# Attention's values in two products a head instead of three, with the dilated half's division on ScalarE

## The chip, the cores and the metric

The kernel runs on one core of a Trainium2 chip. The metric is the device time of one execution in microseconds. The engines are TensorE (PE in the profile, its weight loads PEld), VectorE (DVE), ScalarE (ACT), GpSimd (POOL) and SyncE (SP), which starts DMAs. Each engine takes its own instructions strictly in the order of its list; semaphores tie the lists together.

## The reference

The program is two network blocks, one behind the other, on 512 tokens of width 1024. The change touches the attention of the first block alone: 8 heads of causal attention with a forget gate ("fox") and 8 heads of dilated attention, 64 values wide each. Cut to that part:

```python
proj = rms_norm(h, norm1_g) @ w_in                 # q, k, v of both kinds of heads
# fox, per head: causal softmax over all keys before
s = q @ k.T / 8 + c_q - c_k ; p = softmax(mask(s)) ; fox_out = p @ v
# dilated, per head: three windows (128 by 1, 512 by 4, 2048 by 16), each a softmax
# with an ALiBi bias, mixed by their denominators
o = sum_i softmax_i(lse)[i] * (softmax(s_i) @ v)
h = h + concat(fox_out, dil_out) @ w_out
```

The rest (a layer of 16384 small experts, then retention, convolution and a gated layer) runs behind it and isn't changed.

## The kernel before

**Numbers in two parts.** Products are made in fp32r. So that little is lost, an operand is split in a high part (ScalarE's copy into fp32r) and a low part (the original less the high part, by VectorE or, for some weights, GpSimd), and a product A B is three matmuls: high high, high low, low high. Lines 1351 to 1353 are the three of a projection's weight tile: `wh`, `wl` are a weight's parts (ScalarE makes `wh` from the loaded `raw`, line 2539; `wl` is line 1826 on VectorE or 2941 on GpSimd), `XH` and `XL` those of the normed input.

**Units and groups.** Weights come in units of 128 output features by 1024, 8 tiles of three matmuls each. Units 1 to 24 make q, k, v for eight groups of two heads (groups 0 to 3 are dilated, 4 to 7 fox); units 25 to 32 are the output projection `w_out`, which reads the heads' results from `MH` and `ML` (high and low part, one slot of 512 columns for a group, `place(g)`, 64 partitions for each head).

**Attention beside it.** One generator, `timeline()`, yields the pieces of work; each engine runs through it and issues its share, so the order of every list is fixed when the program is built. Attention is side work: after each tile of the projection a tick lets `attend()` go on by its credit (its yields of 1.4 and 1.35 for the first 34 of its iterations, 1.05 after), that is 2.75 tiles an iteration and later 2.1. It has 64 steps n: group, head, block qb of 128 queries, with 128 (qb + 1) keys. Iteration n issues, in this order:
- `turn_low` of step n-4: VectorE takes the low part of the transposed probabilities into `PTL`, from PSUM, and frees that bank (P4 or P5);
- `scores` n: TensorE, three matmuls into one of three banks;
- `soft` n-1: VectorE adds the mask in place and takes the row minimum (line 1969), ScalarE the exponential into one of five tiles T (line 2668; 2670 for fox heads, which also sums);
- `normal` n-2: VectorE multiplies by the counts of windows that see a key (`CNT`) and sums (line 1979, dilated heads only), takes the reciprocal (line 1983) and multiplies by it (line 1985);
- a tile or two of the projection;
- where step n-5 was the fourth of its head, `values` of that head (lines 1618 to 1632): 12 matmuls into P6, then ScalarE copies 64 rows to `MH` and VectorE takes `ML`;
- `turn` n-3: TensorE transposes the probabilities (line 1358) and ScalarE copies them to `PTH`, the high part;
- a tile or two.

`VV` holds the values of a group's two heads, 4 key blocks of 128 columns (64 for each head), the high part in one tensor, the low part in another; so a product for one head also computes the other head's 64 rows, which nobody reads. The V of a group is copied out of its bank (`v_copy`), transposed (`v_turn`) and split; Q and K are split from their banks (`qk_split`). These pieces stand at the end of units, ahead of or behind `attend()`'s pieces as the ticks fall. `high` and `low` are the weight pieces of units to come, up to four ahead. The waits in the lists: VectorE's low part waits for ScalarE's `PTH` copy (`s_pth`), ScalarE's exponential for VectorE's minimum (`s_min`), the count product for the exponential (`s_exp`), the transposes for the division (`s_soft`), output tiles for `ML` (`s_ml`).

## Time and profile before

| | |
|---|---|
| runs | 2445.4, 2454.4, 2445.06 us; median 2445.4 |
| the profiled execution | 2445.81 us, span 2443.6 us |
| TensorE's granted clock, mean | 0.997 of full speed |
| busy share of the span | TensorE 99%, VectorE 73%, ScalarE 48%, GpSimd 23% |

In the page's 40 slices of 61 us attention lies in the first to the fifth. The granted clock is 90% or more of full speed in each slice. Busy shares are averages over stages with different limits; a wait belongs to the engine named first, and the engine behind the arrow ended it. A matmul's recorded end is modelled and overlaps the next one's start, so distances between starts say more of TensorE than durations.

### The profile page before, as it was taken

How to read it: one execution, taken by the hardware profiler on the slowest of the kernel's cores; microseconds unless marked ns; L12 is line 12 of the kernel's file. 1: busy time of each engine (PE TensorE's matmuls, PEld its weight loads, DVE VectorE, ACT ScalarE, POOL GpSimd, SP SyncE). 2: the span in 40 equal slices, each digit the busy share in tenths (PEclk: the TensorE clock that was granted, in tenths of full speed). 3: DMA queues.
4: the chain of work that ended last, by engine and by line, in shares of the span. 5: the costliest groups of instructions: out<-in, count | busy, mean ns of one | idle time of the engine just before them, and what ended most of it. 6: DMA issues, size and time to landing. Idle time of an engine off the chain costs nothing.

```text
span 2443.6 us, 35669 instructions
## 1 busy us (share of the span) xinstructions
PE 2408.1 (99%) x13533; PEld 2189.5 (90%) x13533; DVE 1781.7 (73%) x3391; ACT 1185.1 (48%) x2193; POOL 564.7 (23%) x372
## 2 busy tenths in 40 slices
PE   8999999999999999999999999999999999999998
PEld 7788888999999999999999998887888888888887
DVE  7876667998998886899999988777785336433323
ACT  6555466478778885333333345445322223332222
POOL 3222065133333541455555510000000000000000
PEclk9999999999999999999999999999999999999999
DMA  4111345699999999999999972222574322222331
GB/s 173 67 57 53 122 147 177 218 325 342 344 336 341 389 405 363 411 412 412 411 407 409 410 286 83 81 87 93 183 250 134 104 87 95 95 98 93 106 101 35
DMA packets 193114, 533.89 MB, mean 218 GB/s; under 512 B 16712, under 2 KB 65896, under 8 KB 190768
## 3 DMA queue, kind: packets, MB, share of 16 engines
q1 hardware_dynamic: 151472, 380.60, 43.3%
q0 software_dynamic: 41472, 151.01, 16.2%
q8 instruction: 108, 1.77, 0.3%
q14 instruction: 62, 0.51, 0.1%
HBM read 480.09 MB, written 51.46 MB: 218 GB/s over the span
## 4 chain that ended last, share of the span: by engine, by line
PE 91%; DVE 4%; ACT 2%; DMA 1%; issue 1%; DVEq 0%; SPq 0%; ACTq 0%
PE P L1351 28%; PE P L1353 28%; PE P L1352 28%; PE P L1716 2%; DMA hdram<-HID 1%; PE P L1358 1%; ACT wh L2539 1%; DVE wl L1826 1%; DVE T L1829 0%; PE P L1631 0%; PE P L1630 0%; PE P L1629 0%; PE P L1608 0%; PE P L1609 0%; PE P L1607 0%
## 5 line engine op out<-in xcount | busy, mean ns | idle before, releaser
L1351 PE MATMUL P<-XH,wh 128*128 128x512 f32 (+2 forms) x2272 | 833.9, 367 | 3.7 <-DVE wl L1826 3.7
L1353 PE MATMUL P<-XH,wl 128*128 128x512 f32 (+2 forms) x2272 | 817.6, 360 | 0.0
L1352 PE MATMUL P<-XL,wh 128*128 128x512 f32 (+2 forms) x2272 | 817.3, 360 | 0.0
L2539 ACT ACTIVATE wh<-raw 128x1024 fp32r<-128x1024 f32 x458 | 482.5, 1056 | 398.4 <-PE P L1353 398.4
L1826 DVE TENSOR_TENSOR wl<-raw,wh 128x1024 fp32r<-128x1024 f32 x422 | 512.6, 1223 | 84.5 <-ACT wh L2539 81.5
L1351 PEld LDWEIGHTS P<-XH,wh 128*128 128x128 f32 x2272 | 428.0, 188 | 48.2 <-DVE wl L1826 4.7
L1353 PEld LDWEIGHTS P<-XH,wl 128*128 128x128 f32 x2272 | 427.4, 188 | 47.6
L1352 PEld LDWEIGHTS P<-XL,wh 128*128 128x128 f32 x2272 | 428.2, 188 | 42.7 <-issue 1.9
L1351 PE MATMUL P<-AH,wh 128*128 128x368 f32 (+1 forms) x1024 | 337.4, 330 | 1.1 <-DVE AL L1826 1.1
L1352 PE MATMUL P<-AL,wh 128*128 128x368 f32 (+1 forms) x1024 | 336.7, 329 | 0.0
L1353 PE MATMUL P<-AH,wl 128*128 128x368 f32 (+1 forms) x1024 | 336.7, 329 | 0.0
L2990 POOL DMA_INDIRECT GV<-vt,SI x128 | 201.3, 1573 | 172.5 <-DVE SUM L1829 152.3
L2981 POOL DMA_INDIRECT GB<-un,SI x116 | 159.3, 1374 | 285.1 <-DVE HS L2172 231.8
L1351 PEld LDWEIGHTS P<-AH,wh 128*128 128x128 f32 x1024 | 192.4, 188 | 1.6 <-issue 1.4
L1352 PEld LDWEIGHTS P<-AL,wh 128*128 128x128 f32 x1024 | 192.4, 188 | 0.0
L1353 PEld LDWEIGHTS P<-AH,wl 128*128 128x128 f32 x1024 | 192.4, 188 | 0.0
L1826 DVE TENSOR_TENSOR T<-P,T 128x512 f32<-128x512 f32 x47 | 32.5, 691 | 197.0 <-PE P L1353 191.8
L1829 DVE SCALAR_TENSOR_TENSOR SUM<-GV,HS,SUM 128x1024 f32<-128x1024 f32 x127 | 162.6, 1281 | 4.0 <-DVE SUM L1829 0.5
L2172 DVE CUSTOM_DVE_ANT_0 GB<-GB,XT 128x1024 f32<-128x1024 f32 x116 | 140.6, 1223 | 14.0 <-DMA GB<-un,SI 13.9
L2752 ACT ACTIVATE OM<-OE,GTL 128x128 f16<-128x128 f16 x368 | 146.2, 436 | 0.0
L2941 POOL TENSOR_TENSOR wl<-raw,wh 128x1024 fp32r<-128x1024 f32 x36 | 86.4, 2399 | 249.5 <-ACT wh L2539 248.0
L2776 ACT ACTIVATE HID<-P 128x368 f32<-128x368 f32 x128 | 60.8, 475 | 95.7 <-PE P L1353 82.7
(345 smaller groups left out, 3393.9 us busy)
## 6 DMA issues: line engine op xcount, KB each, us to landing
raw<-wts SPq DMA_DIRECT2D x211, 512.0 KB
raw<-ut SPq DMA_DIRECT2D x128, 512.0 KB
raw<-vt SPq DMA_DIRECT2D x128, 512.0 KB
hdram<-HID SPq DMA_DIRECT2D x64, 384.0 KB
HI<-hdram SPq DMA_DIRECT2D x32, 768.0 KB
gdram<-GS SPq DMA_DIRECT2D x23, 1024.0 KB
GI<-gdram SPq DMA_DIRECT2D x16, 1472.0 KB
AWC<-adat SPq DMA_DIRECT2D x64, 256.0 KB, 5.4
```

The costliest lines, as they stand in the source:

```text
L1351: e.matmul(bank, wh[:, w], H, start=start, stop=False)
L1352: e.matmul(bank, wh[:, w], L, start=False, stop=False)
L1353: return e.matmul(bank, wl[:, w], H, start=False, stop=stop)
L1826: return e.tensor_tensor(dst, a, b, op)
L1829: return e.scalar_tensor_tensor(out=dst, in0=a, scalar=scalar, in1=b, op0=op0, op1=op1)
L2172: e.tensor_tensor_reduce(out=b[:, :], in0=b[:, :], in1=rows_[:, :], scale=1.0, scalar=0.0, op0=ALU.mult, op1=ALU.add, accum_out=sums[:, k: ...
L2539: return e.activation(dst, src, ACT.Copy)
L2752: t = e.activation(OM[n % 2][:, 1, r, :, o], OE[n % 3][:, 0, r, :, o], ACT.Copy, scale=GTL[n // 32 % 2][:, at_:at_ + 1])
L2776: e.activation(HID[n % 2][:, i % 2, NX:ND], P[i % 4][:, NX:ND], ACT.Gelu).then_inc(s_gelu, 1)
L2941: e.tensor_tensor(WL[i % NW][:, :], RAW[i % NRAW][:, :], WH[i % NW][:, :].bitcast(F32), ALU.subtract).then_inc(s_low_p, 1)
L2981: e.indirect_dma_start(GB[n % 4][:, :], None, un, bass.IndirectOffsetOnAxis(ap=(SIX if extra else SI)[:, k:k + 1], axis=0)).then_inc(d_row ...
L2990: e.indirect_dma_start(GV[n % 6][:, :], None, table, bass.IndirectOffsetOnAxis(ap=(SIX if extra else SI)[:, k:k + 1], axis=0)).then_inc(d_ ...
```

## The change

It has four parts.

1. `VV` becomes `VX`: for each key block and head 64 columns of the high part and, right beside them, 64 of the low part. One wide matmul with both as weights and `PTH` moving gives high high in rows 0 to 63 of P6 and low high in rows 64 to 127; a narrow one with 64 columns of weights and `PTL` moving adds the third product to rows 0 to 63. So 8 matmuls a head. The last head (v = 15) keeps three products, all with 64 columns.
2. The two halves of P6 are added: ScalarE copies rows 0 to 63 to `MS` (tile T5), VectorE adds rows 64 to 127 to it. An iteration later (`values_high`) ScalarE copies `MS` to `MH` and GpSimd subtracts for `ML`. The last head goes the old way.
3. `T5` is now `MS`, so V waits for its transposes in one tile (`T6`) instead of two.
4. For steps of the dilated heads the multiplication by the reciprocal goes from VectorE to ScalarE (`normal` in ScalarE's part, line 2709 in the changed program).

```diff
@@ -361,11 +361,13 @@
                 yield ("soft", n - 1, *steps[n - 1])
             if 0 <= n - 2 < ns:
                 yield ("normal", n - 2, *steps[n - 2])
+            if 0 <= n - 6 < ns and steps[n - 6][2] == 3:
+                yield ("values_high", *steps[n - 6][:2])
+                state["values"] += 1
             yield 1.4 if n < 34 else 1.05
             if 0 <= n - 5 < ns and steps[n - 5][2] == 3:
                 g, h, _ = steps[n - 5]
                 yield ("values", g, h, at[n - 5], v_at[g])
-                state["values"] += 1
             if 0 <= n - 3 < ns:
                 at[n - 3] = tr()
                 yield ("turn", n - 3, *steps[n - 3], at[n - 3])
...
@@ -881,7 +883,7 @@
         MH = at("MH", F + 16, [128, 8, T], F32R)
         ML = at("ML", F + 32, [128, 8, T], F32R)
         QK = [[at(f"QK{g}{i}", F + 48 + 16 * g + 4 * i, [128, 2, T], F32R) for i in range(4)] for g in range(2)]
-        VV = [[at(f"VV{g}{i}", F + 80 + 4 * g + 2 * i, [128, 4, 128], F32R) for i in range(2)] for g in range(2)]
+        VX = [at(f"VX{g}", F + 80 + 4 * g, [128, 4, 2, 2, 64], F32R) for g in range(2)]
         hT = at("hT", F, [128, 8, T], F32)
         adr = nc.dram_tensor("adram", [2, 8, T], F32, kind="Internal").ap()
         cd = nc.dram_tensor("cdram", [2, 8, T], F32, kind="Internal").ap()
...
@@ -956,6 +958,7 @@
         DM = [at(f"DM{i}", F + 94 + 2 * i, [128, T], F32) for i in range(2)]
         RSQ = at("RSQ", F + 98, [128, T], F32)
         R1 = TB[4]
+        MS = TB[5]
 
 
         AWC = [at(f"AWC{i}", F + (16, 18, 20, 22, 28, 30)[i], [128, T], F32) for i in range(6)]
...
@@ -1591,7 +1596,7 @@
                     p.wait_ge(s_tr[t % 2], t // 2)
                 elif t == 0:
                     p.wait_ge(s_fox_v, 1)
-                transposes(P[4 + t % 2], TB[6 - g % 2], 4).then_inc(s_vt, 1)
+                transposes(P[4 + t % 2], TB[6], 4).then_inc(s_vt, 1)
 
             def scores(n, g, h, qb):
                 q = QK[g % 2]
...
@@ -1618,17 +1623,34 @@
             def values(g, h, t, tv):
                 v = 2 * g + h
                 if v:
-                    p.wait_ge(s_ml, v)
+                    p.wait_ge(s_mix, 3 * v - 1)
                 else:
                     p.wait_ge(s_vcopy, 2)
                 p.wait_ge(s_tr[t % 2], t // 2 + 1)
                 p.wait_ge(s_tr[tv % 2], tv // 2 + 1)
-                vh, vl = VV[g % 2]
+                both = VX[g % 2]
                 for kb in range(4):
-                    d = P[6][:, kb * 128:T]
-                    e.matmul(d, vh[:, kb, :], key_row(PTH, v, kb), start=kb == 0, stop=False)
-                    e.matmul(d, vh[:, kb, :], key_row(PTL, v, kb), start=False, stop=False)
-                    m = e.matmul(d, vl[:, kb, :], key_row(PTH, v, kb), start=False, stop=kb == 3)
+                    d = slice(kb * 128, T)
+                    if v < 15:
+                        def wide():
+                            return e.matmul(P[6][:, d], both[:, kb, h, :, :].rearrange("p a b -> p (a b)"),
+                                            key_row(PTH, v, kb), start=kb == 0, stop=kb == 3)
+
+                        def narrow():
+                            return e.matmul(P[6][0:64, d], both[:, kb, h, 0, :], key_row(PTL, v, kb), start=False,
+                                            stop=False)
+
+                        if kb < 3:
+                            wide()
+                            narrow()
+                        else:
+                            narrow()
+                            m = wide()
+                    else:
+                        e.matmul(P[6][0:64, d], both[:, kb, h, 0, :], key_row(PTH, v, kb), start=kb == 0, stop=False)
+                        e.matmul(P[6][0:64, d], both[:, kb, h, 1, :], key_row(PTH, v, kb), start=False, stop=False)
+                        m = e.matmul(P[6][0:64, d], both[:, kb, h, 0, :], key_row(PTL, v, kb), start=False,
+                                     stop=kb == 3)
                 m.then_inc(s_val, 1)
 
             def key(hp):
...
@@ -1954,10 +1976,10 @@
                         tt(L, src, H.bitcast(F32), ALU.subtract).then_inc(s_qkl, 1)
 
             def v_turn(g, t):
-                src = P[4 + t % 2][:, :].rearrange("p (b c) -> p b c", b=4)
-                H, L = VV[g % 2]
+                src = P[4 + t % 2][:, :].rearrange("p (b h c) -> p b h c", b=4, h=2)
                 v.wait_ge(s_vh, g + 1)
-                tt(L[:, :, :], src, H[:, :, :].bitcast(F32), ALU.subtract).then_inc(s_tr[t % 2], 1)
+                tt(VX[g % 2][:, :, :, 1, :], src, VX[g % 2][:, :, :, 0, :].bitcast(F32),
+                   ALU.subtract).then_inc(s_tr[t % 2], 1)
 
             def soft(n, g, h, qb):
                 kw = 128 * (qb + 1)
...
@@ -1981,7 +2003,11 @@
                                                 accum_out=st[:, c + 2:c + 3]).then_inc(s_v, 1))
                     own()
                 step(e.reciprocal(st[:, c + 3:c + 4], st[:, c + 2:c + 3]).then_inc(s_v, 1))
+                divided[n] = step.n
+                if dilated(g):
+                    return
                 own()
+                v.wait_ge(s_soft, 32)
                 e.tensor_scalar(p_[:, 0:kw], p_[:, 0:kw], st[:, c + 3:c + 4], None, ALU.mult).then_inc(s_soft, 1)
 
             def turn_low(n, g, h, qb, t):
...
@@ -1997,9 +2023,14 @@
 
             def values(g, h, t, tv):
                 rows = slice(64 * h, 64 * h + 64)
-                v.wait_ge(s_mh, 2 * g + h + 1)
-                tt(ML[rows, place(g), :], P[6][rows, :], MH[rows, place(g), :].bitcast(F32),
-                   ALU.subtract).then_inc(s_ml, 1)
+                n = 2 * g + h
+                v.wait_ge(s_mix, 3 * n + 1)
+                if n < 15:
+                    tt(MS[rows, :], P[6][64:128, :], MS[rows, :], ALU.add).then_inc(s_mix, 1)
+                else:
+                    v.wait_ge(s_ml, 15)
+                    tt(ML[rows, place(g), :], P[6][0:64, :], MH[rows, place(g), :].bitcast(F32),
+                       ALU.subtract).then_inc(s_ml, 1)
 
             def mixed(m, half):
                 w = cols(half)
...
@@ -2647,15 +2678,15 @@
                     return
                 c.wait_ge(s_used, U_QKV + 3 * g + 3)
                 c.wait_ge(s_fox_v, 1)
-                if g >= 2:
-                    c.wait_ge(s_vt, g - 1)
-                copy(TB[6 - g % 2][:, :], P[qkv_home(g, 2)][:, :]).then_inc(s_vcopy, 1)
+                c.wait_ge(s_vt, g)
+                copy(TB[6][:, :], P[qkv_home(g, 2)][:, :]).then_inc(s_vcopy, 1)
 
             def v_turn(g, t):
                 c.wait_ge(s_vt, g + 1)
                 if g >= 2:
                     c.wait_ge(s_val, 2 * (g - 1))
-                copy(VV[g % 2][0][:, :, :], P[4 + t % 2][:, :].rearrange("p (b c) -> p b c", b=4)).then_inc(s_vh, 1)
+                copy(VX[g % 2][:, :, :, 0, :],
+                     P[4 + t % 2][:, :].rearrange("p (b h c) -> p b h c", b=4, h=2)).then_inc(s_vh, 1)
 
             def soft(n, g, h, qb):
                 kw = 128 * (qb + 1)
...
@@ -2670,6 +2701,14 @@
                     e.activation(dst, src, ACT.Exp, bias=st[:, j:j + 1], scale=-1.0,
                                  accum_out=st[:, j + 2:j + 3]).then_inc(s_exp, 1)
 
+            def normal(n, g, h, qb):
+                if dilated(g):
+                    kw = 128 * (qb + 1)
+                    j = 4 * (n % 4)
+                    c.wait_ge(s_v, divided[n])
+                    e.activation(TB[n % 5][:, 0:kw], TB[n % 5][:, 0:kw], ACT.Copy,
+                                 scale=st[:, j + 3:j + 4]).then_inc(s_soft, 1)
+
             def turn(n, g, h, qb, t):
                 src = P[4 + t % 2][:, 0:128 * (qb + 1)].rearrange("p (k q) -> p k q", q=128)
                 c.wait_ge(s_turn, n + 1)
...
@@ -2682,8 +2721,20 @@
 
             def values(g, h, t, tv):
                 rows = slice(64 * h, 64 * h + 64)
-                c.wait_ge(s_val, 2 * g + h + 1)
-                copy(MH[rows, place(g), :], P[6][rows, :]).then_inc(s_mh, 1)
+                n = 2 * g + h
+                c.wait_ge(s_val, n + 1)
+                if n:
+                    c.wait_ge(s_mix, 3 * n)
+                if n >= 2:
+                    c.wait_ge(s_ml, n - 1)
+                copy(MS[rows, :] if n < 15 else MH[rows, place(g), :], P[6][0:64, :]).then_inc(s_mix, 1)
+
+            def values_high(g, h):
+                rows = slice(64 * h, 64 * h + 64)
+                n = 2 * g + h
+                if n < 15:
+                    c.wait_ge(s_mix, 3 * n + 2)
+                    copy(MH[rows, place(g), :], MS[rows, :]).then_inc(s_mix, 1)
 
 
             def subkeys(i):
...
@@ -2932,6 +2983,8 @@
                 if low_on_pool(i):
                     if "fill" in last:
                         g.wait_ge(s_fill, last["fill"])
+                    if "mix" in last:
+                        g.wait_ge(s_ml, last["mix"])
                     if "part" in last:
                         g.wait_ge(s_mprod, last["part"])
                     g.wait_ge(s_high, i + 1)
...
@@ -2956,11 +3009,24 @@
                         n += 1
                 last["fill"] = n
 
+            def values_high(group, h):
+                rows = slice(64 * h, 64 * h + 64)
+                if (group, h) != (7, 1):
+                    g.wait_ge(s_fill, last["fill"])
+                    g.wait_ge(s_low_p, last["low"])
+                    if group or h:
+                        g.wait_ge(s_ml, 2 * group + h)
+                    g.wait_ge(s_mix, 3 * (2 * group + h + 1))
+                    e.tensor_tensor(ML[rows, place(group), :], MS[rows, :], MH[rows, place(group), :].bitcast(F32),
+                                    ALU.subtract).then_inc(s_ml, 1)
+                    last["mix"] = 2 * group + h + 1
+
             def mod_part(n):
                 if n >= NM:
                     return
                 a, cb, landed, count = mod_home(n)
                 half = mod_part_of(n)[0]
+                g.wait_ge(s_ml, 15)
                 g.wait_ge(s_csil, 1)
                 g.wait_ge(s_low_p, last["low"])
                 g.wait_ge(s_fill, last["fill"])
```

ScalarE's list, from the exponential of step 10 (group 1) to the PTH copy of step 10. T0 to T4 are the exponentials' tiles, T5 is MS, PTH0 the high part for even heads. Before:
```order
L2668 ACTIVATE T0_101<-P3,st_91 128x384 [waits s_min]
L2539 ACTIVATE PTH0_131<-P4 128x128 [waits s_turn]
L2668 ACTIVATE T1_102<-P7,st_91 128x512 [waits s_min]
L2539 ACTIVATE MH_135<-P6 64x512 [waits s_val]
L2539 ACTIVATE PTH0_131<-P5 128x2x128 [waits s_turn]
L2668 ACTIVATE T2_103<-P2,st_91 128x128 [waits s_min]
L2539 ACTIVATE PTH0_131<-P4 128x3x128 [waits s_turn]
```

Now:
```order
L2699 ACTIVATE T0_101<-P3,st_91 128x384 [waits s_min]
L2709 ACTIVATE T4_105<-T4_105,st_91 128x256 [waits s_v]
L2570 ACTIVATE PTH0_131<-P4 128x128 [waits s_turn]
L2699 ACTIVATE T1_102<-P7,st_91 128x512 [waits s_min]
L2709 ACTIVATE T0_101<-T0_101,st_91 128x384 [waits s_v]
L2570 ACTIVATE T5_106<-P6 64x512 [waits s_mix,s_val]
L2570 ACTIVATE PTH0_131<-P5 128x2x128 [waits s_turn]
L2699 ACTIVATE T2_103<-P2,st_91 128x128 [waits s_min]
L2709 ACTIVATE T1_102<-T1_102,st_91 128x512 [waits s_v]
L2570 ACTIVATE MH_135<-T5_106 64x512 [waits s_mix]
L2570 ACTIVATE PTH0_131<-P4 128x3x128 [waits s_turn]
```

Behind each exponential stands the division of the step before it, and the copies to MS and MH stand ahead of the PTH copies.

VectorE's list at the same place, from a low part to the next. The two ISA rows are the row minimum and the count product, each followed by the read of its accumulator. Before:
```order
L1826 TENSOR_TENSOR PTL0_133<-P4,PTH0_131 128x128 [waits s_val,s_pth]
L1969 ISA P7,st_91<-P7,MDB_129 128x512 [waits s_scores]
L1969 ISA st_91 128x1
L1979 ISA T0_101,st_91<-T0_101,CNT_128 128x384 [waits s_exp]
L1979 ISA st_91 128x1
L1983 RECIPROCAL st_91<-st_91 128x1 [waits s_v]
L1985 TENSOR_SCALAR T0_101<-T0_101,st_91 128x384 [waits s_v]
L1826 TENSOR_TENSOR ML_136<-P6,MH_135 64x512 [waits s_mh]
L1826 TENSOR_TENSOR PTL0_133<-P5,PTH0_131 128x2x128 [waits s_pth]
```

Now:
```order
L1848 TENSOR_TENSOR PTL0_133<-P4,PTH0_131 128x128 [waits s_val,s_pth]
L1991 ISA P7,st_91<-P7,MDB_129 128x512 [waits s_scores]
L1991 ISA st_91 128x1
L2001 ISA T0_101,st_91<-T0_101,CNT_128 128x384 [waits s_exp]
L2001 ISA st_91 128x1
L2005 RECIPROCAL st_91<-st_91 128x1 [waits s_v]
L1848 TENSOR_TENSOR T5_106<-P6,T5_106 64x512 [waits s_mix]
L1848 TENSOR_TENSOR PTL0_133<-P5,PTH0_131 128x2x128 [waits s_pth]
```

The division is gone, the sum with MS (T5) stands where ML was made, and the low part that follows waits for the PTH copy as before.

TensorE's list, the values of head 1 (P6 is the bank; P0 is a projection's). Before, where VV00 is the high and VV01 the low part:
```order
L1629 MATMUL P6<-PTH1_132,VV00_145 128x512 [waits s_tr1,s_ml]
L1630 MATMUL P6<-PTL1_134,VV00_145 128x512
L1631 MATMUL P6<-PTH1_132,VV01_146 128x512
L1629 MATMUL P6<-PTH1_132,VV00_145 128x384
L1630 MATMUL P6<-PTL1_134,VV00_145 128x384
L1631 MATMUL P6<-PTH1_132,VV01_146 128x384
L1629 MATMUL P6<-PTH1_132,VV00_145 128x256
L1630 MATMUL P6<-PTL1_134,VV00_145 128x256
L1631 MATMUL P6<-PTH1_132,VV01_146 128x256
L1629 MATMUL P6<-PTH1_132,VV00_145 128x128
L1630 MATMUL P6<-PTL1_134,VV00_145 128x128
L1631 MATMUL P6<-PTH1_132,VV01_146 128x128
```

Now, the eight matmuls of that head:
```order
L1636 MATMUL P6<-PTH1_132,VX0_145 128x512 [waits s_tr1,s_mix]
L1640 MATMUL P6<-PTL1_134,VX0_145 64x512
L1636 MATMUL P6<-PTH1_132,VX0_145 128x384
L1640 MATMUL P6<-PTL1_134,VX0_145 64x384
L1636 MATMUL P6<-PTH1_132,VX0_145 128x256
L1640 MATMUL P6<-PTL1_134,VX0_145 64x256
L1640 MATMUL P6<-PTL1_134,VX0_145 64x128
L1636 MATMUL P6<-PTH1_132,VX0_145 128x128
```

The order of all other pieces on TensorE is the same. The wide products write 128 rows, the narrow ones 64.

## Rows read from the trace of the kernel before

**Rows 1.** the page, engines: busy us, share, instructions
```profile
PE 2408.1 (99%) x13533; PEld 2189.5 (90%) x13533; DVE 1781.7 (73%) x3391; ACT 1185.1 (48%) x2193; POOL 564.7 (23%) x372
```

**Rows 2.** windows: stretch, length, busy of each engine (count), PEclk, DMA share, GB/s
```profile
60.00:175.00 115.00, 111.67 (x599) 93.48 (x598) 98.42 (x273) 60.51 (x122) 28.76 (x12) 1.00 0.18 61
175.00:262.00 87.00, 86.31 (x466) 73.31 (x465) 55.67 (x154) 46.16 (x111) 19.12 (x8) 1.00 0.16 50
```

**Rows 3.** waits from 60 to 175 us: total us, times, longest
```profile
ACT T L2668 <- DVE st L1969: 40.7, 27, 3.0
...
PEld P L1358 <- DVE T L1985: 5.5, 9, 1.2
```

**Rows 4.** VectorE's groups, 28 steps: count, busy us, mean ns, idle before
```profile
L1979 DVE CUSTOM_DVE_ANT_0 T<-T,CNT 128x128 f32<-128x128 f32 (+3 forms) x28 | 23.7, 845 | 0.0
L1985 DVE TENSOR_SCALAR T<-T,st 128x128 f32<-128x128 f32 (+3 forms) x29 | 15.0, 518 | 1.0
L1826 DVE TENSOR_TENSOR PTL<-P,PTH 128x512 fp32r<-128x512 f32 (+3 forms) x28 | 13.6, 487 | 3.5 <-ACT PTH L2539 3.3
L1969 DVE CUSTOM_DVE_ANT_0 P<-P,MDB 128x384 f32<-128x384 f32 (+3 forms) x26 | 13.0, 499 | 0.0
```

**Rows 5.** ScalarE's groups, the same 28 steps
```profile
L2668 ACT ACTIVATE T<-P,st 128x384 f32<-128x384 f32 (+3 forms) x26 | 14.0, 537 | 37.2 <-DVE st L1969 37.2
L2539 ACT ACTIVATE PTH<-P 128x128 fp32r<-128x128 f32 (+3 forms) x28 | 12.1, 431 | 0.9 <-PE P L1358 0.7
```

**Rows 6.** timeline of VectorE, one step: start us, duration us, what
```profile
94.72 0.69 DVE L1979 CUSTOM_DVE_ANT_0 T<-T,CNT 128x512 f32<-128x512 f32 x1
...
95.45 0.16 DVE L1983 RECIPROCAL st<-st 128x1 f32<-128x1 f32 x1
95.65 0.49 DVE L1985 TENSOR_SCALAR T<-T,st 128x512 f32<-128x512 f32 x1
96.05 0.55 DVE L1826 TENSOR_TENSOR PTL<-P,PTH 128x384 fp32r<-128x384 f32 x1
```

**Rows 7.** timeline of ScalarE and VectorE at a unit's end
```profile
75.15 0.27 ACT L2539 ACTIVATE PTH<-P 128x128 fp32r<-128x128 f32 x1
...
75.31 0.60 ACT L2539 ACTIVATE VV<-P 128x512 fp32r<-128x512 f32 x1
...
75.78 1.21 ACT L2641 ACTIVATE QK<-P 64x512 fp32r<-64x512 f32 x2
...
76.89 1.05 ACT L2539 ACTIVATE wh<-raw 128x1024 fp32r<-128x1024 f32 x1
...
77.97 0.29 DVE L1826 TENSOR_TENSOR PTL<-P,PTH 128x128 fp32r<-128x128 f32 x1
```

**Rows 8.** timeline, GpSimd beside VectorE's count product
```profile
107.86 2.38 POOL L2941 TENSOR_TENSOR wl<-raw,wh 128x1024 fp32r<-128x1024 f32 x1 [8.31 <-ACT wh L2539]
...
108.35 2.44 DVE L1979 CUSTOM_DVE_ANT_0 T<-T,CNT 128x512 f32<-128x512 f32 x1
```

**Rows 9.** timeline of ScalarE, PTH copies of the fourth and the 32nd step
```profile
72.12 0.59 ACT L2539 ACTIVATE PTH<-P 128x512 fp32r<-128x512 f32 x1
...
165.18 0.60 ACT L2539 ACTIVATE PTH<-P 128x512 fp32r<-128x512 f32 x1
```

**Rows 10.** timeline of TensorE, the values of one head and what follows
```profile
129.90 0.40 PE L1629 MATMUL P<-PTH,VV 128*128 128x512 f32 x1
129.90 0.19 PEld L1630 LDWEIGHTS P<-PTL,VV 128*128 128x128 f32 x1
130.13 0.39 PE L1630 MATMUL P<-PTL,VV 128*128 128x512 f32 x1
...
131.76 0.41 PE L1358 MATMUL P<-ident,T 128*128 128x128 f32 x2
...
131.93 0.48 PE L1351 MATMUL P<-XH,wh 128*128 128x512 f32 x1
...
132.25 0.40 PE L1352 MATMUL P<-XL,wh 128*128 128x512 f32 x1
```

9 lines of the change are left out of this document (5 added, 4 removed).

## The prediction

> **What bounds the kernel now.** I read the page first: TensorE is busy 99% of the span [rows 1]. So a matmul that goes is worth its time only where no other engine is about to take over. The change touches attention alone, which runs as side work between the projection's matmuls, so I cut its stretch out by windows [rows 2]. The 32 steps of the dilated half (a step is one block of 128 queries of one head, four to a head) are over before 175 us; the other 32 follow. From 60 to 175 us VectorE is busy 98.4 of 115 us beside TensorE's 111.7; from 175 to 262 it is busy 55.7 of 87, and TensorE 86.3. The table of waits [rows 3] says who sets the pace in the first half: ScalarE waited 27 times, 40.7 us in all, for VectorE's row minimum, and the weight load of the transposes waited 5.5 us for VectorE's division. So here VectorE's ordered list and TensorE are nearly level. After 175 us TensorE alone binds. Two stretches, two limits; the change has to be priced in each.
>
> **Matmuls removed.** A head's values cost 12 matmuls: for each of four key blocks 512, 384, 256 and 128 columns, three products. From the first (129.90) to the transposes behind the last (131.76) is 1.86 us [rows 10]. Of three equal columns one goes, so 0.62 us a head, for 15 heads (the last keeps three): 9.3 us, if a narrow product issues like a wide one. The narrow ones write 64 partitions, and no row of before has such a matmul. In a head the shape changes six times (wide, narrow, wide, narrow, wide, narrow twice, wide, and back). Nothing at all for a change is one end. The other is a drained array: a matmul takes 0.40 us and the next of its kind starts 0.23 us later, so 0.17 us is overlapped and would be lost each time. Between them stands what a change of kind costs today: the first tile matmul behind the fp32 transposes is followed by the next after 0.32 us instead of 0.23 [rows 10], 0.09 more. I take 0.09: six make 0.54, and a head saves 0.08 us net. The ends are 0.62 saved and 0.40 lost. A narrow weight load could also be shorter than a wide one; that would only help, and is inside the low end.
>
> The Trainium skill, TensorEngine Tiling (Array Packing), section Key Properties, says that changing the tiling mode drains TensorE. By that rule the cost is the upper end, by the row it is half of it. No matmul of before has another tile than 128 by 128, so the trace can't decide; it is my third case below.
>
> **The division moved to ScalarE.** VectorE loses 32 divisions (0.518 us mean in this stretch [rows 4]), 16.6 us. By busy time all fits: ScalarE is busy 60.5 of 115 us [rows 2] and gets 32 scalings, plus a copy more per head. That is the tempting sum, and I don't use it, since both engines take their instructions in order. The order rows show a loop that closes once per step: VectorE's low part of step n-4, the minimum of n-1, the count product and sum of n-2, its reciprocal; then ScalarE's division of n-2, and behind it in its list the copy of the transposed block n-3 (PTH); then VectorE's low part of n-3, which waits for that copy. Before, the copy stood behind the exponential only, and ran while VectorE did count, reciprocal and division. Now the two engines alternate. The loop, by the means of the stretch from the PTH copy of the fourth step to that of the 32nd, 28 steps, each less what the next instruction overlaps (about 0.09 on VectorE, 95.65 plus 0.49 against 96.05 [rows 6]; about 0.10 on ScalarE, 75.15 plus 0.27 against 75.31 [rows 7]):
> low part 0.487 less 0.09, 0.40; minimum 0.499 less 0.09, 0.41 [rows 4]; count with its accumulator read 0.499 (the same sizes as the minimum, undisturbed) plus 0.04, as 94.72 to 95.45 for one of 0.69 [rows 6], 0.53; reciprocal to the start of the next 0.20 [rows 6]; the division on ScalarE, for which I take the exponential's 0.537, since both read a scale or bias per partition, less 0.10, 0.44; the PTH copy 0.43 [rows 5]. Together 2.41 us, times 28: 67.5.
>
> What stands in the loop beside it:
> - The count product waits while GpSimd runs: it took 2.44 us at 108.35 with GpSimd's subtraction from 107.86 for 2.38 [rows 8]. Its mean is 0.845 against 0.499, so 28 times 0.346, 9.7 us. The 15 new subtractions on GpSimd are half as long (1.2 us each) and follow the MH copy, with a PTH copy, a low part and a minimum (0.43, 0.40, 0.41) before the next count: they are over by then. Nothing.
> - The copy of the values' upper half to MS stands between division and PTH copy, 0.5 us, and VectorE's addition (0.6) before its low part runs past the PTH copy by 0.2. Seven times 0.7, 4.9 us.
> - The new copy MS to MH stands there too: seven times 0.5, 3.5 us. I take the 0.60 of the V copy [rows 7], less 0.10, for both.
> - At a unit's end the V and Q or K copies and their low parts come between: from the PTH copy's end (75.42) to the next low part (77.97) 2.55 us [rows 7]. Four of these, less a little where they overlap, 10.0; three without V, each 0.5 less, 6.0; three times a V copy and a weight copy (1.05), of which 0.4, 0.3 and, where they come ahead of the PTH copy, 1.5 show: 2.2. Together 18.2.
>
> Sum: 67.5 + 9.7 + 4.9 + 3.5 + 18.2 = 103.8 us. The same 28 steps take 93.06 us now, from 72.12 to 165.18 [rows 9]. The loop is later by 10.7 us. TensorE may run ahead of it by somewhat more than now, since it needs the division and not the PTH copy, less than half a step of 3.3 us; I choose 1.0 us for that and take 9.7. What TensorE saves in heads 0 to 7 is hidden under it, and so is the cost of narrow matmuls there.
>
> **The later half.** Heads 8 to 14 keep VectorE's division and TensorE binds: 7 times 0.62 saved less 0.54, 0.6 us. The low part of the values now comes from GpSimd behind two more steps (addition, copy, subtraction: 0.6, 0.6, 1.2 us), and output tiles wait for it. By the order four steps lie between head 13's values and the first tile that needs them, each with two tiles of three matmuls at 0.23 us, so at least 5.5 us against these 2.4: covered. The one home for V before its transposes, and P6 released by the addition instead of the subtraction, wait for nothing new: these are a unit and a head apart. If cover failed at the last output tiles, each would cost 1 to 2 us.
>
> Before's profiled execution took 2445.81 us (span 2443.6, 2.2 around it), the runs shown have a median of 2445.4. So 2445.8 + 9.7 - 0.6 = 2454.9.
>
> **Rivals.**
> First, TensorE stays the bound throughout, the offload does what busy time promises. For it: VectorE loses 16.6 us and TensorE's waits for it. Against it: the loop above, of which every piece is a row. Then 15 heads give 9.3 with free narrow matmuls and the waits for VectorE (about 3.3 us of matmul time, inside the 111.67 of 115) go: 2433.2. With 0.09 a change it is 15 times 0.08 and 3.3: 2441.3.
> Second, narrow products cost more than they save: a drained array in the second half, where nothing covers it. Per head 6 times 0.17 less 0.62, 0.40 lost; 7 heads lose 2.8 and the sum is 2458.3. If the weight load of 0.19 [rows 10] is exposed as well, a head loses 6 times 0.36 less 0.62, 1.54, and 7 heads 10.8: 2466.3. It turns against the change from 0.10 us a change on. For it: nothing else in the program has such tiles, so the array is set anew each time. Against it: weight loads run ahead of matmuls everywhere in this trace.
> By the same skill page this second case would be the rule, at 2458.3.
>
> **How the numbers follow.** The loop binds with cheap or moderate changes of shape, 2447 to 2462: 0.50. First rival, 2433 to 2442: 0.26. Second, 2458 to 2467: 0.20. Something else: 0.04. The likeliest gives 2454.9. The range 2436 to 2464 leaves out the best part of the first and the worst of the second. A measurement can tell about 0.5% here, 12.2 us, so faster means under 2433.2 and slower above 2457.6. Faster: a third of the first rival and little else, 0.10. Slower: nearly all of the second and a fifth of the forecast's own cases, 0.29. Same: 0.61.
>
> **What would show it.** If the loop binds: the fourth and the 32nd PTH copy stand 100 to 107 us apart instead of 93; ScalarE waits for VectorE's reciprocal in most of 32 steps; VectorE waits for PTH copies (3.5 us in these 28 steps now [rows 4]) 20 us and more, though it is less busy; transposes wait, now for ScalarE's division. If the distance is 90 or less, the step on the loop is wrong. The price of a change of shape is read from the starts of a head's eight matmuls after 175 us: 1.24 us for all says free, 1.8 says 0.09, 2.3 a drain. Count products with means near 0.845 confirm the GpSimd term; much longer ones would say that the new subtractions hit them.

## The result, and the profile after

| | before | after |
|---|---|---|
| median of 6 runs | 2445.67 us | 2460.58 us |
| lowest and highest | 2445.06, 2454.4 | 2458.28, 2463.38 |
| profiled execution, its span | 2445.81, 2443.6 | 2460.08, 2458.2 |

The changed kernel is slower: the ratio after to before is 1.0057, 95% interval [1.0045, 1.0069]. The forecast was 2454.9 us with a range of 2436 to 2464.

The page of the changed kernel, engines (busy us, share, instructions), answers to [rows 1]. VectorE lost 19 us of work, ScalarE gained 25 and GpSimd 21, and the kernel is slower: a sum of busy time doesn't tell it.

```profile
PE 2404.0 (98%) x13473; PEld 2179.3 (89%) x13473; DVE 1762.3 (72%) x3359; ACT 1209.9 (49%) x2240; POOL 585.4 (24%) x387
```

The windows of the changed kernel, the same stretches as in [rows 2] (length, busy of each engine with its count, PEclk, DMA share, GB/s):

```profile
60.00:175.00 115.00, 100.39 (x520) 80.31 (x519) 69.45 (x219) 75.13 (x146) 35.46 (x18) 1.00 0.16 52
175.00:262.00 87.00, 80.42 (x421) 65.37 (x420) 58.56 (x152) 48.88 (x115) 29.29 (x15) 1.00 0.17 55
```

In the first stretch no engine is the bound by its busy time any more: TensorE fell from 111.67 to 100.39, VectorE from 98.42 to 69.45. They wait for each other. (The stretch is cut by time, so in the slower kernel it also holds a little less of the work.) In the second TensorE idles 6.6 of 87 us, where it idled 0.7. The table of waits of the changed kernel from 60 to 175 us (total, times, longest) names the pairs and answers to [rows 3]:

```profile
ACT T L2699 <- DVE st L1991: 28.9, 27, 1.3
DVE PTL L1848 <- ACT PTH L2570: 27.5, 21, 2.2
...
PEld P L1363 <- ACT T L2709: 12.3, 13, 2.3
...
PE P L1363 <- ACT T L2709: 7.6, 7, 1.9
DVE T L1848 <- ACT T L2570: 8.0, 7, 1.3
ACT T L2709 <- DVE st L2005: 6.1, 11, 1.9
PE P L1363 <- DVE PTL L1848: 5.8, 4, 2.6
```

VectorE waits for ScalarE's PTH copy, 21 times, and ScalarE for VectorE's minimum, 27 times: the alternation. Line 2709 is the new division, for which the transposes (line 1363) now wait. It waits itself for VectorE's reciprocal only 11 times, where the prediction had named most of 32 steps as a sign; in the others ScalarE itself was still busy when the reciprocal was done. The groups of VectorE and ScalarE from 74.97 to 175 us (columns as in [rows 4, 5]):

```profile
L2001 DVE CUSTOM_DVE_ANT_0 T<-T,CNT 128x256 f32<-128x256 f32 (+3 forms) x27 | 15.5, 575 | 0.0
L1848 DVE TENSOR_TENSOR PTL<-P,PTH 128x512 fp32r<-128x512 f32 (+3 forms) x28 | 13.8, 491 | 23.1 <-ACT PTH L2570 22.8
```
```profile
L2709 ACT ACTIVATE T<-T,st 128x256 f32<-128x256 f32 (+3 forms) x27 | 15.3, 568 | 4.5 <-DVE st L2005 4.5
L2570 ACT ACTIVATE PTH<-P 128x512 fp32r<-128x512 f32 (+3 forms) x29 | 12.5, 430 | 0.2
```

The count product's mean fell from 845 to 575 ns, which I had not foreseen. The two PTH copies that answer to [rows 9], of the fourth and the 32nd step (timeline of ScalarE: start, duration, what):

```profile
74.39 0.58 ACT L2570 ACTIVATE PTH<-P 128x512 fp32r<-128x512 f32 x1
```
```profile
174.39 0.60 ACT L2570 ACTIVATE PTH<-P 128x512 fp32r<-128x512 f32 x1
```

They are 100.0 us apart; they were 93.06. The map of the whole loss is made from the start of each head's first values matmul and of the stores of HID in the stage behind attention (64 of them, of which the first starts at 415.09 us before):

| | before | after | difference |
|---|---|---|---|
| head 0's values start | 76.60 | 78.03 | +1.4 |
| head 0 to head 7 (dilated half) | 90.46 | 97.83 | +7.4 |
| head 7 to head 14 (fox half) | 89.60 | 92.65 | +3.1 |
| head 14 to the first store of HID | 158.43 | 157.46 | -1.0 |
| first to last store of HID | 556.62 | 560.41 | +3.8 |
| last store to the end of the span | 1471.9 | 1471.8 | -0.1 |

Three places lose: the dilated half, the fox half, which should have won, and the stage of small experts, which the change doesn't touch (e7 and e8 below take that one up).

The chain in the dilated half can be read off two timelines, ScalarE and VectorE of the changed kernel around 147 us:

```profile
147.31 0.58 ACT L2699 ACTIVATE T<-P,st 128x384 f32<-128x384 f32 x1 [1.29 <-DVE st L1991]
147.79 0.51 ACT L2709 ACTIVATE T<-T,st 128x256 f32<-128x256 f32 x1
148.21 0.26 ACT L2570 ACTIVATE PTH<-P 128x128 fp32r<-128x128 f32 x1
149.49 0.69 ACT L2699 ACTIVATE T<-P,st 128x512 f32<-128x512 f32 x1 [1.02 <-DVE st L1991]
```
```profile
146.05 0.69 DVE L1848 TENSOR_TENSOR PTL<-P,PTH 128x512 fp32r<-128x512 f32 x1 [0.96 <-ACT PTH L2570]
146.66 0.56 DVE L1991 CUSTOM_DVE_ANT_0 P<-P,MDB 128x384 f32<-128x384 f32 x1
...
147.59 0.17 DVE L2005 RECIPROCAL st<-st 128x1 f32<-128x1 f32 x1
148.50 0.29 DVE L1848 TENSOR_TENSOR PTL<-P,PTH 128x128 fp32r<-128x128 f32 x1 [0.74 <-ACT PTH L2570]
```

Low part 146.05, minimum 146.66, exponential 147.31, division 147.79, PTH copy 148.21, next low part 148.50. Each starts when the one before it is done, across two engines; on one engine the next starts up to 0.10 us before the recorded end. The reciprocal ends at 147.76, just ahead of the division, so here both branches, exponential and reciprocal, are equally long. Before, the division was not in this chain for ScalarE.

TensorE's timeline of head 8's values in the changed kernel (one wide and one narrow product for each key block) prices the change of shape:

```profile
190.80 0.39 PE L1636 MATMUL P<-PTH,VX 128*128 128x512 f32 x1
191.02 0.40 PE L1640 MATMUL P<-PTL,VX 128*64 128x512 f32 x1
191.26 0.33 PE L1636 MATMUL P<-PTH,VX 128*128 128x384 f32 x1
...
191.90 0.28 PE L1636 MATMUL P<-PTH,VX 128*128 128x128 f32 x1
192.01 0.41 PE L1363 MATMUL P<-ident,T 128*128 128x128 f32 x2
```

1.21 us from the first to the transposes, where 12 products took 1.86 [rows 10]: 0.65 saved, nothing for the changes.

The fox half's loss, the changed kernel's GpSimd, VectorE and TensorE around 209 us:

```profile
207.51 1.29 POOL L3020 TENSOR_TENSOR ML<-T,MH 64x512 fp32r<-64x512 f32 x1 [8.29 <-ACT MH L2570]
208.87 2.36 POOL L2994 TENSOR_TENSOR wl<-raw,wh 128x1024 fp32r<-128x1024 f32 x1
```
```profile
207.92 0.56 DVE L1848 TENSOR_TENSOR PTL<-P,PTH 128x384 fp32r<-128x384 f32 x1 [1.15 <-ACT PTH L2570]
208.39 0.42 DVE L1991 CUSTOM_DVE_ANT_0 P<-P,MCB 128x256 f32<-128x256 f32 x1
...
208.93 2.38 DVE L2011 TENSOR_SCALAR T<-T,st 128x128 f32<-128x128 f32 x1
```
```profile
211.37 0.33 PE L1363 MATMUL P<-ident,T 128*128 128x128 f32 x1 [1.63 <-DVE T L2011]
```

GpSimd waits 8.29 us for the MH copy, subtracts ML, and only then takes the weight's low part (`wl`), which stood behind it in its list; the ScalarE copy `wh` that it needs had begun at 201.31 and took 1.05 us. That falls on a division of 128 columns, which takes 2.38 us (one at 202.41 us in `e4_both_v`, beside no GpSimd work, takes 0.29), and TensorE idles 1.63 for it. VectorE's low part and minimum, which read PSUM, ran at full speed beside the ML subtraction. The Trainium skill, SBUF — State Buffer, section Who interferes with whom, has it as a rule: one port pair is shared by the two engines, a scaling from SBUF to SBUF can take it, and the one that comes second is blocked for the other's whole instruction. The rows agree, with 2.38 beside GpSimd's 2.36: the division ends 0.08 us after GpSimd's instruction.

### The profile page after: what moved, and what is told of

It is laid out like the page before. It is cut to its first block, busy times and chain, and to the rows that moved or that the text cites. A ratio compares the mean times of both kernels' runs of the same rounds, so it can differ in the third digit from the quotient of the medians.

```text
span 2458.2 us, 35611 instructions
## 1 busy us (share of the span) xinstructions
PE 2404.0 (98%) x13473; PEld 2179.3 (89%) x13473; DVE 1762.3 (72%) x3359; ACT 1209.9 (49%) x2240; POOL 585.4 (24%) x387
## 3 DMA queue, kind: packets, MB, share of 16 engines
q8 instruction: 107, 1.75, 0.3%
## 4 chain that ended last, share of the span: by engine, by line
PE 86%; DVE 7%; ACT 5%; issue 1%; DMA 1%; DVEq 0%; SPq 0%; ACTq 0%
PE P L1356 27%; PE P L1358 27%; PE P L1357 27%; PE P L1738 2%; DVE PTL L1848 1%; ACT wh L2570 1%; DVE P L1991 1%; DMA hdram<-HID 1%; DVE T L1848 1%; PE P L1363 1%; ACT PTH L2570 1%; DVE wl L1848 1%; DVE T L1851 0%; ACT T L2709 0%; ACT T L2699 0%
## 5 line engine op out<-in xcount | busy, mean ns | idle before, releaser
L1848 DVE TENSOR_TENSOR T<-P,T 128x512 f32<-128x512 f32 (+1 forms) x62 | 42.9, 691 | 215.2 <-PE P L1358 191.8
```

Of the source, the lines that this page charges most:

```text
L1848: return e.tensor_tensor(dst, a, b, op)
```

## The experiments

Ten runs. e7 and e8 are one execution each and have their own section; the other eight stand in one table, with medians of 5 (e2, e3) or 11 executions; "28 steps" is the distance of the PTH copies of the fourth and the 32nd step.

| run | median us | ratio to before, 95% | head 0 starts | 28 steps | heads 0-7 | heads 7-14 |
|---|---|---|---|---|---|---|
| before | 2445.67 | | 76.60 | 93.06 | 90.46 | 89.60 |
| after | 2460.58 | 1.0057 [1.0045, 1.0069] | 78.03 | 100.00 | 97.83 | 92.65 |
| e1_div_v | 2449.12 | 1.0007 [0.9998, 1.0016] | 75.71 | 92.12 | 89.12 | 92.70 |
| e2_div_a | 2459.81 | 1.0058 [1.0044, 1.0071] | 78.25 | 102.73 | 100.57 | 89.70 |
| e3_low_v | 2468.95 | 1.0085 [1.0071, 1.0099] | 79.20 | 108.73 | 107.63 | 88.82 |
| e4_both_v | 2452.44 | 1.0021 [1.0012, 1.0030] | 75.88 | 96.78 | 93.77 | 89.47 |
| e5_hybrid | 2447.72 | 1.0005 [0.9996, 1.0014] | 76.28 | 92.06 | 89.06 | 89.81 |
| e6_div_late | 2452.45 | 1.0022 [1.0013, 1.0031] | 79.67 | 91.04 | 87.69 | 92.64 |
| e9_before_div_late | 2452.01 | 1.0020 [1.0011, 1.0029] | 80.41 | 95.65 | 91.99 | 89.60 |
| e10_joined | 2445.13 | 0.9988 [0.9979, 0.9997] | 76.86 | 90.27 | 87.82 | 89.82 |

The kernel before had medians of 2446.58 (e1 to e4), 2446.17 (e5, e6) and 2447.29 (e9, e10) beside them.

### e1_div_v: the division back on VectorE

VectorE's part of the edit; ScalarE's `normal` goes as a whole:

```diff
...
-                if dilated(g):
-                    return
                 own()
-                v.wait_ge(s_soft, 32)
                 e.tensor_scalar(p_[:, 0:kw], p_[:, 0:kw], st[:, c + 3:c + 4], None, ALU.mult).then_inc(s_soft, 1)
```

> The changed kernel with the dilated half's division back on VectorE; the values still in two products. Theory 1 (the round trip VectorE, ScalarE, VectorE in each dilated step carries the loss there): the first values product of head 7 starts near 169 us (167.06 before, 175.86 after the change), the PTH copies of steps 4 and 32 lie 94 to 96 us apart (93.06, then 100.0), and the time falls by 5 to 8 us to 2452.5 to 2455.5. Rival (the new work at a head's end, MS copy, add, MH copy and GpSimd's subtraction, carries it): the distance stays at 98 us or more, and the time at 2458 or above. The fox half (start of head 7 to start of head 14: 89.60 before, 92.65 after) is the same as after under both.

Measured: 28 steps in 92.12 us and 2449.12 us, both below what theory 1 expected (94 to 96, 2452.5 to 2455.5). The 7.9 us between this and after are the division's, all in the dilated half; the head ends, which both kernels have, carry none of it. The fox half keeps its loss (92.70). VectorE's groups of this kernel from 73 to 167 us:

```profile
L2007 DVE TENSOR_SCALAR T<-T,st 128x256 f32<-128x256 f32 (+3 forms) x29 | 22.3, 770 | 1.0
L2001 DVE CUSTOM_DVE_ANT_0 T<-T,CNT 128x256 f32<-128x256 f32 (+3 forms) x27 | 15.0, 554 | 0.0
```

GpSimd's stall has moved: the count product is near its undisturbed 0.50 us, the division went from 518 [rows 4] to 770. It depends on where GpSimd's subtraction happens to start, and in the changed kernel, where VectorE has no division in these steps, it falls mostly on nothing.

### e2_div_a: the division alone

The kernel before, with ScalarE's division in the changed kernel's place, ahead of the PTH copy:

```diff
+            def normal(n, g, h, qb):            # ScalarE
+                if dilated(g):
...
+                    c.wait_ge(s_v, divided[n])
+                    e.activation(TB[n % 5][:, 0:kw], TB[n % 5][:, 0:kw], ACT.Copy,
+                                 scale=st[:, j + 3:j + 4]).then_inc(s_soft, 1)
```

> The kernel before with only the dilated half's division moved to ScalarE; the values in three products as before. Theory 1: the loop alone is slow, PTH copies of steps 4 and 32 97 to 100 us apart, head 7 starts at 171 to 174 us, the fox half keeps its 89.6 us, and the time is 2449.5 to 2453. Rival (the work at a head's end carries the loss): distance 93 to 94, VectorE is freed of 15 us and nothing is late, time 2444 to 2447.

Measured: 2459.81 us, 28 steps in 102.73, the fox half untouched. Theory 1 in kind, and much larger than it said: the offload of the division alone loses as much as the whole change, 13.2 us on its own runs of before. So the two products give something back in the dilated half (100.57 against 97.83), although they add work at the head ends, and the difference that fits is the count product: 575 ns there, here 845 (28 times 0.27 is 7.6 us, of which the head ends take a part back).

### e3_low_v: the low part on VectorE

```diff
+            def values_low(g, h):               # VectorE, behind `turn` in the iteration of the MH copy
...
+                v.wait_ge(s_mix, 3 * n + 3)
+                tt(ML[rows, place(g), :], MS[rows, :], MH[rows, place(g), :].bitcast(F32), ALU.subtract)
...
-            def values_high(group, h):          # GpSimd
```

> The changed kernel with the low part of the 15 heads (ML) subtracted by VectorE, one step after the MH copy, in place of GpSimd. Theory 2 (in the fox half GpSimd's 1.29 us subtraction and the 2.4 us of a weight's low part queued behind it hold up VectorE's division): heads 7 to 14 take 86 to 88 us (92.65 after, 89.60 before; their eight heads less 0.65 each would be 85.1), the fox division's mean returns from 695 to about 585 ns, and the time is 2453 to 2456. Rival (the fox half loses by the copies and adds at a head's end themselves, which stay here and gain one more on VectorE): heads 7 to 14 take 92 us or more, time 2459 to 2463. In the dilated half the count product should lengthen again from 575 to some 800 ns, as the low parts of weights return to their old places, and add up to 6 us there if the loop is what bounds.

Measured: the slowest of all, 2468.95, where theory 2 said 2453 to 2456. It was wrong on the dilated half: 28 steps in 108.73 instead of 100.0. It had named up to 6 us for this and left them out of its time. The count product's mean over these steps is back at 854 ns (28 times 0.28 is 7.8 us). The seven ML of 0.69 on VectorE add little: a head without a unit's end takes 11.66 us from PTH copy to PTH copy, 0.2 more than in the changed kernel. On the fox half it was right in kind and not in size: 88.82 instead of 92.65, where it said 86 to 88. The division there, from 187 to 276 us of this kernel:

```profile
L2013 DVE TENSOR_SCALAR T<-T,st 128x384 f32<-128x384 f32 (+3 forms) x28 | 16.5, 590 | 1.2
```

The changed kernel has 682 ns there (168 to 270 us). Its TensorE waited three times for that division, 4.4 us; here not at all.

### e4_both_v: division and low part on VectorE

The edits of e1_div_v and e3_low_v together.

> The changed kernel with both: division and low part on VectorE. What is left of the change is the two products a head, one more copy on ScalarE and one add on VectorE. Theories 1 and 2 together: head 7 starts at 168 to 170 us, heads 7 to 14 take 86 to 88, time 2443 to 2447, no gain or a small one over before since the dilated half gives back what the fox half saves. Rival (head ends carry the loss): 2453 or more.

Measured: head 7 at 169.65, the fox half 89.47, 2452.44 us. Neither the forecast (2443 to 2447) nor, by a hair, the rival (2453). What I had missed is that the dilated half is VectorE's again and pays for the add and ML (93.77 against 90.46). Against e1_div_v it isolates who makes ML: GpSimd is better by 4.7 us in the dilated half, VectorE by 3.2 in the fox half.

Of the 4.55 us that seven heads save, the fox half shows next to nothing here. Two of the seven heads, at 193.77 and 220.44 us, took 2.23 and 2.18 us to the next other matmul instead of 1.21: by the table of waits TensorE waited for VectorE's low part, twice, 1.3 us. TensorE's idle time in this half is 2.9 us (89.47 less 86.54 busy), before it was 0.7 (89.60 less 88.91). So waits take back at least half of what the products save; where the rest goes, and which new work causes each wait, wasn't tested.

### e5_hybrid: each half with its better maker of ML

Division on VectorE; ML by GpSimd for heads 0 to 6, by VectorE from head 7 (`values_low` as in e3_low_v). The line that decides:

```diff
-                if (group, h) != (7, 1):        # GpSimd
+                if 2 * group + h < 7:
```

> Two products a head, division on VectorE, and the low part of the heads' values (ML) subtracted by GpSimd for the seven dilated heads 0 to 6 and by VectorE for heads 7 to 14. It joins the half of e1_div_v that was best (start of head 0 to head 7 89.12 us) with the half of e4_both_v that was best (head 7 to head 14 89.47 us). If the two halves add, head 14 starts at 254 to 255 us (256.66 before), and the time is 2444 to 2449, about that of before, since the stage from 816 to 963 us has cost the kernels with two products 3 to 5 us more in their traces. Rival (the halves aren't independent: TensorE owes the work that the first half put off): the second half takes 91 us or more and the time is 2449 or above.

Measured: 89.06 and 89.81, head 14 at 255.15, 2447.72 us. The halves add, and this is before's time within the interval.

### e6_div_late: the same work in another order

```diff
-            def normal(n, g, h, qb):            # ScalarE
+            def divide(n, g, h, qb):            # ScalarE
...
                 yield ("turn", n - 3, *steps[n - 3], at[n - 3])
+            if 0 <= n - 2 < ns:
+                yield ("divide", n - 2, *steps[n - 2])
```

> The changed kernel, all its parts kept, with ScalarE's division of step n-2 put behind the PTH copy of step n-3 in each step. Theory 1 (the division costs because it stands on the one chain subtraction of a row, minimum, exponential, division, PTH copy, next subtraction): with the copy ahead of it, the division runs beside VectorE's subtraction and minimum; 28 times up to 0.5 us leave the chain, until TensorE bounds: PTH copies of steps 4 and 32 90 to 95 us apart (100.0 after, 93.06 before), head 7 starts at 167 to 171 us, time 2449 to 2455. Rival (what costs is the amount of work, or the later division itself, for which TensorE's transposes then wait): distance 98 or more, time 2459 or above.

Measured: 28 steps in 91.04 us instead of 100.0, with every instruction of the changed kernel kept. This is the experiment on which I rest the cause: an order alone takes the whole loss of the dilated half away and 2 us more. GpSimd's stalls did not move with it: the count product's mean over the 28 steps is 579 ns, in the changed kernel 575. The quiet steps of a head (no unit's end in them) take 2.84 + 2.62 + 2.50 + 1.99 = 9.95 us from PTH copy to PTH copy, in the changed kernel 2.77 + 2.90 + 3.61 + 2.18 = 11.46. ScalarE's timeline of this kernel around 155 us:

```profile
154.82 0.28 ACT L2572 ACTIVATE PTH<-P 128x128 fp32r<-128x128 f32 x1
154.98 0.52 ACT L2711 ACTIVATE T<-T,st 128x256 f32<-128x256 f32 x1
156.12 0.69 ACT L2701 ACTIVATE T<-P,st 128x512 f32<-128x512 f32 x1 [0.63 <-DVE st L1993]
```
```profile
155.13 0.29 DVE L1850 TENSOR_TENSOR PTL<-P,PTH 128x128 fp32r<-128x128 f32 x1 [1.71 <-ACT PTH L2572]
155.34 0.69 DVE L1993 CUSTOM_DVE_ANT_0 P<-P,MDB 128x512 f32<-128x512 f32 x1
```

The division (154.98) now lies beside VectorE's low part and minimum (155.13, 155.34). The first head starts late, 79.67 against 78.03, since the first divisions come later.

### e7_before_again and e8_after_again: two more traces

> The kernel before once more, for a second trace. From the 47th of the 64 stores of HID (816 us) to the last (971.7 us) the kernel before took 155 us; the kernels with two products took 3.5 to 5.1 us more, all with the same instructions there. If that is chance of the moment (transfers at 400 GB/s, gathers), this trace differs from the first by some us; if it belongs to the kernel, it is within 0.5 us of it.

> The changed kernel once more, for a second trace. From the 47th store of HID to the last: 158 us in the first trace, 3.1 us more than before. If that is chance, it differs here by 1 us or more; if it belongs to the kernel, it doesn't. The attention stage up to 426 us should repeat within 0.3 us.

Measured: attention repeats. Before 90.45 and 89.60, first store of HID at 414.47; after 97.79 and 92.64, first store at 426.63. Both begin up to 0.7 us away from their first trace, so the first store misses the 0.3 us that was expected, and the halves themselves repeat within 0.04.

The second trace of after also tests whether TensorE binds in the dilated half. Behind a wait of 1.89 us for ScalarE's division, from 157.6 to 161.0 us, its granted clock was 0.50, the lower level of 1.2 GHz (columns as in [rows 2]; in the first trace the clock is 1.00 there):

```profile
157.60:161.00 3.40, 3.40 (x11) 2.63 (x10) 1.78 (x7) 1.81 (x5) 3.10 (x2) 0.50 0.00 0
```

Its matmuls of 512 columns start 0.43 us apart there instead of 0.23, and heads 0 to 7 took 97.79 us all the same, against 97.83. So TensorE isn't the bound at that place.

In the stage of small experts the second trace of before took 3.3 us more than the first from first to last store (2.3 of it from 816 us on), nearly as much as most kernels with two products, and the second of after 4.1 more than the first of before. So the first trace of before was a lucky one. Between the two traces of after the stretch from the 47th store on differs by 0.8 us, a little under the 1 us that the expectation had asked for. TensorE's waits from 816 to 980 us, before and before again:

```profile
PE P L1716 <- ACT OM L2752: 2.6, 2, 2.1
```
```profile
PE P L1716 <- ACT OM L2752: 3.9, 2, 3.0
PE P L1716 <- issue: 1.3, 1, 1.3
```

And the windows of the same two traces from 865 to 885 us:

```profile
865.00:885.00 20.00, 19.52 (x148) 19.02 (x148) 17.07 (x26) 18.75 (x51) 10.24 (x8) 1.00 1.05 403
865.00:885.00 20.00, 16.83 (x111) 16.57 (x112) 14.95 (x23) 18.52 (x50) 7.32 (x6) 0.91 1.05 397
```

The two executions took 2448.45 and 2461.52 us. The stage, in which transfers run at some 400 GB/s and rows are gathered, has two courses. In one TensorE waits 3.0 us in one piece for ScalarE's `OM`, at 866 to 888 us, and its granted clock is 0.50 for 3.4 or 6.8 us right there; the 64 stores then take 559.9 to 562.1 us. In the other that wait is 0.5 to 2.1 us, the clock stays at 1.00 there, and the stores take 556.6 to 558.1. The second trace of before and seven of the eight traces with two products (all but `e5_hybrid`) took the long course; before, `e2_div_a`, `e9_before_div_late` and `e5_hybrid` took the short one. So neither course belongs to one kind of kernel, but whether the change makes the long one more frequent, these twelve traces don't settle. What starts the long wait stays open.

### e9_before_div_late: the late division without the two products

> The kernel before, values in three products, with the dilated division moved to ScalarE as in e2_div_a but behind the PTH copy. It differs from e2_div_a in that order alone. Theory 1 (the order makes the chain): heads 0 to 7 take 88 to 92 us (e2_div_a 100.57, before 90.46), the fox half its 89.7 us; head 0 starts some 3 us late as in e6_div_late, so that head 7 starts at 168 to 171 us and the time is 2447 to 2451. Rival (the late division was good in e6_div_late only since the two products had freed TensorE, or since GpSimd's stalls had moved): 95 us or more, time 2454 or above.

Measured: 28 steps in 95.65 us (e2_div_a 102.73), heads 0 to 7 in 91.99, at the edge of what was expected, the fox half 89.60. Head 0 starts at 80.41, 3.8 us late where 3 were expected, so head 7 starts at 172.40 (168 to 171 expected) and the time is 2452.01 us, one microsecond above. The order is worth 7.1 us here, so e6_div_late wasn't good only through the two products. But without them the division on ScalarE doesn't pay at all (95.65 against 93.06 before); the count product stays at 854 ns.

### e10_joined: what the runs point to

Two products, late division on ScalarE from the fifth step on, ML by GpSimd up to head 6 and by VectorE from head 7. The new part of the edit:

```diff
+                if 4 <= n and dilated(g):       # ScalarE divides, behind the PTH copy
+                    if n == 4:
+                        c.wait_ge(s_soft, 4)
```

> What the runs so far point to, joined: two products a head, ScalarE's division behind the PTH copy (but on VectorE in the first four steps, where it started head 0 some 1.5 us later), the low part by GpSimd for heads 0 to 6 and by VectorE from head 7 on. If the parts add: head 0 starts at 76 to 78 us, heads 0 to 7 take 87.7 us, heads 7 to 14 take 89.5, so head 14 starts at 253.5 to 255.5 (256.66 before, 268.51 after) and the time is 2443 to 2446.5 against 2446 for before. Rival (they don't add: what the dilated half saves, VectorE and TensorE owe to the fox half): head 14 at 257 or later and 2448 or above.

Measured: head 0 at 76.86, 87.82 and 89.82, head 14 at 254.50; 2445.13 us, ratio 0.9988 [0.9979, 0.9997]. It is faster than before by a tenth of a per cent, which is little beside 0.5% but outside its interval, and faster than the changed kernel by about 15 us. Its eleven executions lie between 2441.64 and 2447.5 us, a spread wider than the gain. Head 14 starts 2.2 us earlier than before (254.50, 256.66), as much as the median gains. The parts add.

## Why the prediction came out as it did

**The mechanism held.** The loop binds: the 28 steps take 100.0 us, VectorE waits 22.8 us for PTH copies in them though it is less busy, and transposes wait for ScalarE's division. The first rival (TensorE stays the bound, 2433 to 2441) is out by e2_div_a and by the halved clock of e8_after_again, the second (narrow products drain the array) by TensorE's timeline. One sign failed: the wait for the reciprocal, 11 times instead of in most of 32 steps.

**The sum was right partly by terms that cancel.** 103.8 us were forecast for the 28 steps.
- GpSimd's stalls, 9.7 us, did not stay: this was the term furthest off. 28 times (0.575 - 0.500) leaves 2.1. I had asked whether the new subtractions would hit the count product. The other question, where the low parts of weights land when they queue behind ML, I had not asked; it decides this term, and its opposite in the fox half.
- The head ends, 1.2 us each, were too cheap. ScalarE's rows of the changed kernel at two head ends:

```profile
109.05 0.62 ACT L2709 ACTIVATE T<-T,st 128x384 f32<-128x384 f32 x1
109.58 0.57 ACT L2570 ACTIVATE T<-P 64x512 f32<-64x512 f32 x1
110.05 0.36 ACT L2570 ACTIVATE PTH<-P 128x256 fp32r<-128x256 f32 x1
```
```profile
98.35 0.72 ACT L2709 ACTIVATE T<-T,st 128x512 f32<-128x512 f32 x1 [0.39 <-DVE st L2005]
99.09 0.63 ACT L2570 ACTIVATE MH<-T 64x512 fp32r<-64x512 f32 x1
99.75 0.49 ACT L2570 ACTIVATE PTH<-P 128x384 fp32r<-128x384 f32 x1
```

  The copy to MS puts the PTH copy off by 0.47 us (109.58 to 110.05), the copy to MH by 0.78 (without it the PTH copy would start 0.10 ahead of the division's end, at 98.97, and it starts at 99.75), and VectorE's addition puts the low part off by 0.32: together 1.57. Over even and odd heads it is 1.5 to 1.8, so some 3 us more than forecast in seven heads.
- The bare step was nearly right: 2.41 us forecast. The quiet steps of the changed kernel, 11.46 us for four, less this 1.57 leave 9.89, that is 2.47 a step. In e2_div_a they are 2.77, 3.15, 2.84 and 2.16, together 10.92; less its own MH copy (0.73) and VectorE's ML (0.31) they leave 2.47 too. So 0.06 more, 1.7 us in 28 steps.
- What is left for the ends of units is some 17 us, where 18.2 were forecast.
- Head 0 started 1.4 us late, ahead of the 28 steps, which was in no term. The 1.0 us by which TensorE was to run ahead of the loop did not show: heads 0 to 7 lose 7.4 us, the 28 steps 6.9.

These are estimates from single rows. They say that the 103.8 us came near the measured 100.0 since the stalls were 7.6 us too dear and head ends and bare step together some 5 too cheap.

The dilated half with this start is +8.8 where I had 9.7.

**The change of shape** I priced at 0.09 us; it is nothing. In this kernel wide and narrow products alternate at 1.21 us for eight, where 2.3 would have said a drain. The Trainium skill, TensorEngine Tiling (Array Packing), section Key Properties, has a change of tiling mode drain the engine. If going from 128 to 64 columns of weights counts as such a change, the trace does not agree.

**The fox half failed in sign.** The step that failed is that "the low part of the values now comes from GpSimd" is "covered", with -0.6 us for the half. I had only looked at who waits for ML. What counts is what GpSimd holds up while it runs: measured +3.1 us in the changed kernel, e1_div_v and e6_div_late alike (92.64 to 92.70), and 88.8 to 89.8 wherever VectorE makes ML. Even there at most 0.8 of the 4.55 us that seven heads save shows against before's 89.60.

**The rest of the distance.** The spans of the profiled pair differ by 14.6 us where I had 9.1: 3.7 more in the fox half, 0.9 less in the dilated one, 1.0 less behind head 14, and 3.8 in the stage of small experts, where the first pair happened to take its two different courses. That the total lay so near the forecast is in part luck: in the dilated half two errors cancel, and the range, 2436 to 2464, was wide. Between the second traces, both on the long course, the spans differ by 13.0 us (2446.2, 2459.2), 12.2 of it by the first store of HID.

## What to carry to other kernels

An offload to an idle engine is priced by the chain, not by busy time: before moving an instruction, write down which of its neighbours in the new engine's list now wait through it. Where two engines hand each other work every step, put what the other engine waits for ahead of what it doesn't; here that order alone was worth 9 us of 100. And when GpSimd gets new work that waits, follow what queues behind it, and which VectorE instructions it will then fall upon.
